# The delta rule's output norm and the out projection of the even layer in one block, the attention's four slices of the contraction first

## The chip, the cores and the metric

The kernel runs on one core of a Trainium2 chip. The time is that of the device for one execution, in microseconds; every comparison is of medians of several executions of the same program.

## The reference, cut to what matters

Two residual layers over a sequence of 1024 tokens of width 1024, all in float32. The even layer ends like this:

```python
def even_layer(x, norm_g, w_in, conv_w, a_log, dt_bias, out_norm, q_gain, k_gain, sinks, w_out, band_bias):
    ...
    o_a = gated_delta_rule(q_a, k_a, v_a, beta_l.astype(F32), alpha_l.astype(F32),
                           a_log.astype(F32), dt_bias.astype(F32))
    o_a = rms_norm(o_a, out_norm) * jax.nn.silu(z_a.astype(F32)).reshape(bsz, T, GDN_HEADS, GDN_HEAD_DIM)
    o_b = sliding_window_attention(...)
    o_b = o_b * jax.nn.silu(z_b.astype(F32))
    mixed = jnp.concatenate([o_a.reshape(bsz, T, BRANCH_WIDTH), o_b], axis=-1).astype(x.dtype)
    return x + mixed @ w_out
```

The delta rule has four heads of 128 channels, the attention eight heads of 64. So `mixed` has 1024 channels: 512 of the delta rule, which need a norm over each head's 128 channels and a gate, and 512 of the attention, which are finished long before. The product with `w_out` sums over all 1024.

## The kernel before

Features lie with channels on the 128 partitions and the 1024 tokens along the free dimension. "Slice" means 128 of the 1024 channels over which the out projection sums; there are eight, `mixed[k]`: four of the delta rule (`v`) and four of the attention (`zb`). A product of float32 operands is made of three passes (L167 to L169) with a high and a low part of each side. For the out projection, ScalarE rounds a slice of the features to its high part (`mh`, L1557) and a slice of the weights to its high part (`wh`, in the tile `xt_hi`, L1559); GpSimd subtracts to get the features' low part (`ml`, L1565), VectorE to get the weights' low part (`wl`, in `xt_lo`, L1596). Each of these is one operation on 128x1024 elements.

The program is a row of blocks. A block holds one list of instructions for each engine, and the next block begins on all engines when the last instruction of the block before is done. Within a block engines wait for each other by semaphores; each engine takes its own list strictly in order. Three blocks matter here:

- `gdn_state` (L1203), the delta rule's recurrence over eight chunks: short matmuls that wait for VectorE and ScalarE in turn. Its last product is the output `o`, which is `v`.
- `norm_blocks` (L612) with tag "eo", the norm of `v`. ScalarE squares the four slices (L655), TensorE sums the squares over the partitions (L675), ScalarE takes the root of the sums (L657), VectorE the reciprocal (L694); the result, one row for each head, is split in a high part (ScalarE, L660) and a low part (VectorE, L698), four operations of 128x256 each; TensorE spreads the rows over 128 partitions by matmuls with a column of ones (L686, L687), two for each half of 512 tokens; and VectorE multiplies slice, gain and the spread row in PSUM (L704). GpSimd meanwhile multiplies the slices with their gates (L666). PSUM has eight banks: bank 0 takes the sums, banks 2 to 7 the spread rows of three slices. At the block's start SP loads the first three rows of weights.
- `project_out` (L1507) with tag "eout". For the first four tiles of 128 tokens the loop over the slices is outside: with slice k ready, TensorE adds its products for tiles 0 to 3 (8 banks, 24 matmuls of 128x512 with all three passes). Then tiles 4 to 7 follow, each with all eight slices. VectorE adds the residual to a finished tile (L1601) and SP stores it. SP loads the weights' rows 3 to 7 one after another into three slots as these come free.

The odd layer's out projection is the same function with `early=4`: it runs beside the end of another computation, which needs two banks, so the first four slices are applied to three tiles only, and tile 3 catches up later.

Where several programs share a block (`side_by_side`, L335), each yields numbers, its due times, and `in_turn` (L308) writes out on each engine whichever is due next:

```python
def in_turn(eng, *programs):
    ...
    while min(due, default=NEVER) < NEVER:
        i = due.index(min(due))
        due[i] = next(steps[i], NEVER)
```

The numbers set the order of an engine's list and nothing else.

## Time and profile before

| | us |
|---|---|
| median of 3 runs | 1574.04 |
| lowest, highest | 1573.94, 1577.53 |
| profiled execution | 1572.04 |
| its span of instructions | 1570.3 |
| mean granted clock of TensorE | 0.897 of full |

The time of an execution is its span and about 1.7 us around it. In the profile PE is TensorE's matmul side, PEld its loading of weights, DVE is VectorE, ACT ScalarE, POOL GpSimd, SP the engine that issues transfers. "PE busy" counts matmuls at whatever clock was granted, so a long busy time is no proof of speed: the clock stands beside it. Matmuls overlap, so the distance between two starts, not the duration of one, is what a matmul costs in a stream. An operation's duration on DVE and POOL includes the time for which it stood waiting after it was issued.

### The profile page before, as it was taken

The numbers are of one execution on the slowest core, as the hardware profiler recorded it, in microseconds if no ns is written. First come the engines' busy times: TensorE is split into PE (matmuls) and PEld (weight loads), VectorE is DVE, ScalarE is ACT, GpSimd is POOL, SyncE is SP. The second block draws the span as 40 slices with busy tenths as digits, with TensorE's granted clock in tenths as the row PEclk, the third lists the DMA queues.
The fourth block names the chain that finished last, engine by engine and source line by source line (L and its number), as shares of the span: only waits on it lengthen the run. The fifth ranks groups of instructions, "written<-read, shape, count | busy, mean of one in ns | idle before, by whom it ended". The sixth has DMA issues, their size and how long they took to land. (4 is left out here: it accounts for less than half of the span.)

```text
span 1570.3 us, 20457 instructions
## 1 busy us (share of the span) xinstructions
PE 1321.9 (84%) x8434; PEld 1102.5 (70%) x8434; DVE 913.7 (58%) x1230; ACT 458.0 (29%) x670; POOL 322.1 (21%) x164
## 2 busy tenths in 40 slices
PE   4999999899568869967997999999432789999698
PEld 4677888678357747856886888887221688988587
DVE  5277745810477446127977464953679777355841
ACT  5234353231333233024342211221652311212310
POOL 2222212121055226013221111121200400000330
PEclk9999999899788989989999999999665666879899
DMA  5212112220400012434241343322000000010423
GB/s 178 42 41 64 44 44 81 68 81 1 154 1 1 1 58 91 147 122 116 81 118 64 102 102 123 86 67 81 0 1 1 1 1 1 2 55 1 188 68 120
DMA packets 118708, 101.96 MB, mean 65 GB/s; under 512 B 37144, under 2 KB 102808, under 8 KB 118488
## 3 DMA queue, kind: packets, MB, share of 16 engines
q1 hardware_dynamic: 104984, 81.65, 17.3%
q10 hardware_dynamic: 13632, 19.01, 3.7%
q8 instruction: 66, 1.08, 0.3%
q14 instruction: 26, 0.21, 0.0%
HBM read 74.43 MB, written 24.51 MB: 63 GB/s over the span
## 5 line engine op out<-in xcount | busy, mean ns | idle before, releaser
L167 PE MATMUL banks<-xt_lo,w_hi 128*128 128x512 f32 x816 | 322.9, 396 | 6.5 <-POOL w_lo L488 6.5
L169 PE MATMUL banks<-xt_hi,w_hi 128*128 128x512 f32 x816 | 319.1, 391 | 0.0
L168 PE MATMUL banks<-xt_hi,w_lo 128*128 128x512 f32 x816 | 319.1, 391 | 0.0
L488 POOL TENSOR_TENSOR w_lo<-features,w_hi 128x1024 fp32r<-128x1024 f32 x55 | 149.0, 2711 | 527.3 <-ACT w_hi L497 527.3
L167 PEld LDWEIGHTS banks<-xt_lo,w_hi 128*128 128x128 f32 x816 | 154.2, 189 | 42.0 <-POOL w_lo L488 7.0
L169 PEld LDWEIGHTS banks<-xt_hi,w_hi 128*128 128x128 f32 x816 | 154.0, 189 | 32.6
L168 PEld LDWEIGHTS banks<-xt_hi,w_lo 128*128 128x128 f32 x816 | 154.4, 189 | 31.3
L541 ACT ACTIVATE temporaries<-banks 128x1024 f32<-128x1024 f32 x47 | 56.0, 1192 | 327.0 <-PE banks L169 318.8
L1601 DVE TENSOR_TENSOR temporaries<-temporaries,banks 128x1024 f32<-128x1024 f32 x16 | 19.5, 1221 | 109.5 <-PE banks L169 100.8
L286 PE MATMUL banks<-temporaries,features 128*128 128x128 f32 x256 | 37.5, 309 | 36.1 <-DVE temporaries L263 36.1
L497 ACT ACTIVATE w_hi<-features 128x1024 fp32r<-128x1024 f32 x55 | 57.8, 1054 | 27.9 <-PE banks L169 26.7
L286 PEld LDWEIGHTS banks<-temporaries,features 128*128 128x128 f32 x256 | 34.8, 220 | 38.8 <-DVE temporaries L263 38.8
L167 PE MATMUL banks<-xt_lo,oout_mh 128*128 128x512 f32 x128 | 51.3, 401 | 11.6 <-DVE xt_lo L1596 11.5
L167 PE MATMUL banks<-xt_lo,eout_mh 128*128 128x512 f32 x128 | 50.9, 398 | 6.8 <-DVE xt_lo L1596 6.8
L2478 DVE COPY_PREDICATED big<-constants,banks 128x384 f32<-128x384 int32 x64 | 34.3, 578 | 32.1 <-PE banks L2418 31.6
L168 PE MATMUL banks<-xt_hi,oout_ml 128*128 128x512 f32 x128 | 51.0, 398 | 0.0
L169 PE MATMUL banks<-xt_hi,oout_mh 128*128 128x512 f32 x128 | 50.8, 397 | 0.0
L168 PE MATMUL banks<-xt_hi,eout_ml 128*128 128x512 f32 x128 | 50.8, 396 | 0.0
L169 PE MATMUL banks<-xt_hi,eout_mh 128*128 128x512 f32 x128 | 50.6, 395 | 0.0
L2418 PE MATMUL banks<-features 64*128 64x128 f32 x384 | 48.9, 332 | 0.0
L588 DVE TENSOR_TENSOR features<-temporaries 128x1024 f32<-128x1024 f32 x13 | 15.9, 1225 | 56.4 <-ACT temporaries L541 56.4
L1596 DVE TENSOR_TENSOR xt_lo<-features,xt_hi 128x1024 fp32r<-128x1024 f32 x16 | 45.5, 2896 | 4.4 <-ACT xt_hi L1559 4.4
(445 smaller groups left out, 2657.8 us busy)
## 6 DMA issues: line engine op xcount, KB each, us to landing
features<-in_even_w_in SPq DMA_DIRECT2D x26, 512.0 KB, 3.9
features<-in_odd_w_in SPq DMA_DIRECT2D x25, 512.0 KB, 4.6
features<-in_x SPq DMA_DIRECT2D x8, 512.0 KB, 7.4
even_gates<-temporaries ACTq DMA_DIRECT2D x8, 512.0 KB, 2.6
features<-even_gates SPq DMA_DIRECT2D x8, 512.0 KB, 8.9
features<-in_even_w_out SPq DMA_DIRECT2D x8, 512.0 KB, 3.5
temporaries<-in_x SPq DMA_DIRECT2D x8, 512.0 KB, 4.0
h_between_layers<-temporaries SPq DMA_DIRECT2D x8, 512.0 KB, 4.1
```

What stands on the lines that cost most here:

```text
L167: nc.tensor.matmul(out, w[0], x[1], start=start, stop=False)
L168: nc.tensor.matmul(out, w[1], x[0], start=False, stop=False)
L169: return nc.tensor.matmul(out, w[0], x[0], start=False, stop=stop)
L286: last = nc.tensor.matmul(co.ps[:, n % 8, k * P:(k + 1) * P], ring[i % deep][:, (4 * h + k) * P:(4 * h + k + 1) * P], diagonal[i % 4], sta ...
L488: nc.gpsimd.tensor_tensor(wl[n % 2], wr[n % NW], wh[n % 2].bitcast(F32), ALU.subtract).then_inc(low, 1)
L497: nc.scalar.activation(wh[n % 2], wr[n % NW], ACT.Copy).then_inc(high, 1)
L541: nc.scalar.activation(to, mine, ACT.Copy, scale=0.5 if kind in ("gate", "turned_gate") else 1.0).then_inc(evacuated, 1)
L588: link(nc.vector.tensor_tensor(dst, x[:, 3:3 + T], x[:, 4:4 + T], ALU.subtract))
L1596: nc.vector.tensor_tensor(wl[:, k, :], wr[k % 3], wh[:, k, :].bitcast(F32), ALU.subtract).then_inc(low_w, 1)
L1601: nc.vector.tensor_tensor(rr[t % 3], rr[t % 3], co.ps[:, 2 * (t % 4):2 * (t % 4) + 2, :].rearrange("p b n -> p (b n)"), ALU.add).then_inc( ...
L2418: last = nc.tensor.matmul(scores(h)[:, i * P:(i + 1) * P], key[rows, j, ct], query[rows, j, ct], start=True, stop=True)
L2478: nc.vector.copy_predicated(x.ring[c % 2][:, h, :, :], mask, scores(h).rearrange("p (s t) -> p s t", s=3)).then_inc(kept, 1)
```

## The change

The block of the norm is gone. A new program `delta_norm` does the same norm inside the block of the out projection. For this:

- the contraction runs over the attention's slices first (`zb + v`, with the rows of `w_out` in the matching order, `first_row`), and the delta rule's slices wait until `delta_norm` has written all eight halves of `v`;
- `project_out` now always works as the odd layer's did: the first four slices go to tiles 0 to 2, in banks 0 to 5, and tile 3 catches up at slice 4. The due times of the first four slices are an argument: `NORM_PACES` in the even layer; `FINISH_PACES` in the odd one, with the numbers that stood in the code;
- `delta_norm` has banks 6 and 7 alone: bank 6 for the sums, then both for the spread rows, a half of 512 tokens in each, so VectorE's last multiplication is split in two halves of 128x512 and TensorE waits for a half before it spreads the next but one;
- squares and rows lie where the weights lay (`A_F[4]`), the weights in `A_F[3]`, which is free once the attention is done, so their first three rows are loaded at the start of `gdn_state`;
- a conversion of the constant `pairs` (L692), which only norms over 64 channels need, is not repeated.

```diff
-def gdn_state(co):
+def gdn_state(co, ahead):
...
+        @block.sync
+        def _(sp):
+            for to, src, sem in ahead:
+                sp.dma_start(to, src).then_inc(sem, 16)
...
-def project_out(co, tag, w, mixed, hi_at, lo_at, res, dst, stored, fetched=False, fetch=(), early=KT, ready=None):
+NORM_PACES = dict(scalar=(0, 4, 7, 9), gpsimd=(0, 4, 7, 10), tensor=(3, 8, 13, 14), vector=(1, 5, 7, 10))
+FINISH_PACES = dict(scalar=(5, 7.5, 10, 12.5), gpsimd=(5, 7.5, 10, 12.5), tensor=(8, 11.5, 15, 18.5), vector=(6, 9.5, 11, 15.5))
+def delta_norm(co, x, gain, gate):
...
+    nc = co.nc
+    Q, N = T // 4, WB
+    here = A_F[4]
+    sq = [co.at(here + 1024 * i, (T,)) for i in range(N)]
+    high, low = (co.rounded(f"eo_rows_{n}", here + 2048 + 1024 * i, (T,)) for i, n in enumerate(("hi", "lo")))
+    rows = co.at(here, (Q,))
+    scale, eps = (co.at(A_CST + C_PARAM + 2 + i, (1,)) for i in range(2))
+    own_quarter = co.at(A_CST + C_QUARTER, (4,))
+    quarters = [(slice(32 * q, 32 * q + 32), slice(Q * q, Q * q + Q)) for q in range(4)]
+    squared, summed, rooted, inverted, high_r, low_r, spread, gated = (
+        co.sem(f"eo_{n}") for n in ("squared", "summed", "rooted", "inverted", "high_r", "low_r", "spread", "gated"))
+    co.delta_normed = normed = co.sem("eo_normed")
+    def scalar(act):
+        yield 1
+        for n in range(N):
+            nc.scalar.activation(sq[n], x[n], ACT.Square).then_inc(squared, 1)
+        yield 8
+        act.wait_ge(summed, N)
+        nc.scalar.activation(rows, co.ps[:, 6, 0:Q], ACT.Sqrt, bias=eps, scale=scale).then_inc(rooted, 1)
+        yield 11
+        act.wait_ge(inverted, 1)
+        for q, (_, of) in enumerate(quarters):
+            nc.scalar.activation(high[:, of], rows, ACT.Copy, scale=own_quarter[:, q:q + 1]).then_inc(high_r, 1)
+    def gpsimd(pool):
+        for n in range(N):
+            yield 2 if n < 2 else 5
+            pool.wait_ge(squared, n + 1)
+            nc.gpsimd.tensor_tensor(x[n], x[n], gate[n], ALU.mult).then_inc(gated, 1)
+    def tensor(pe):
+        yield 4
+        for n in range(N):
+            pe.wait_ge(squared, n + 1)
+            for own, of in quarters:
+                last = nc.tensor.matmul(co.ps[own, 6, 0:Q], co.at(A_CST + C_SUM + 31 - n, (32,)), sq[n][:, of], start=n == 0, stop=n == N - 1)
+            last.then_inc(summed, 1)
+        yield 12
+        pe.wait_ge(low_r, 4)
+        for n in range(N):
+            for h in range(2):
+                if n >= 1:
+                    pe.wait_ge(normed, 2 * n - 1 + h)
+                hs = slice(512 * h, 512 * h + 512)
+                spreader = co.hot_r[:, n:n + 1].to_broadcast([P, P])
+                nc.tensor.matmul(co.ps[:, 6 + h, :], spreader, low[:, hs], start=True, stop=False)
+                nc.tensor.matmul(co.ps[:, 6 + h, :], spreader, high[:, hs], start=False, stop=True).then_inc(spread, 1)
+    def vector(dve):
+        yield 9
+        dve.wait_ge(rooted, 1)
+        nc.vector.reciprocal(rows, rows).then_inc(inverted, 1)
+        yield 11
+        dve.wait_ge(inverted, 1)
+        for q, (_, of) in enumerate(quarters):
+            dve.wait_ge(high_r, q + 1)
+            nc.vector.scalar_tensor_tensor(low[:, of], rows, own_quarter[:, q:q + 1], high[:, of].bitcast(F32), ALU.mult, ALU.subtract).then_inc(low_r, 1)
+        yield 12
+        for n in range(N):
+            dve.wait_ge(gated, n + 1)
+            for h in range(2):
+                hs = slice(512 * h, 512 * h + 512)
+                dve.wait_ge(spread, 2 * n + h + 1)
+                nc.vector.scalar_tensor_tensor(x[n][:, hs], x[n][:, hs], gain, co.ps[:, 6 + h, :], ALU.mult, ALU.mult).then_inc(normed, 1)
+    return dict(scalar=scalar, gpsimd=gpsimd, tensor=tensor, vector=vector)
...
+def project_out(co, tag, w, mixed, hi_at, lo_at, res, dst, stored, paces, ready, w_at, first_row=0, fetched=False, fetch=()):
...
-    wr = [co.at(A_F[4] + 1024 * i, (D,)) for i in range(3)]
+    wr = [co.at(w_at + 1024 * i, (D,)) for i in range(3)]
     rr = [co.at(A_T + 1024 * i, (D,)) for i in range(3)]
+    early = WB
+    w_rows = [slice((first_row + k * P) % D, (first_row + k * P) % D + P) for k in range(KT)]
...
-                sp.dma_start(wr[k], w[k * P:(k + 1) * P, :]).then_inc(loaded[k], 16)
+                sp.dma_start(wr[k], w[w_rows[k], :]).then_inc(loaded[k], 16)
...
-            sp.dma_start(wr[k % 3], w[k * P:(k + 1) * P, :]).then_inc(loaded[k % 3], 16)
+            sp.dma_start(wr[k % 3], w[w_rows[k], :]).then_inc(loaded[k % 3], 16)
...
-            yield 5 + 2.5 * k if k < early else base + k
+            yield paces["scalar"][k] if k < early else base + k
...
-            yield 5 + 2.5 * k if k < early else base + k
+            yield paces["gpsimd"][k] if k < early else base + k
...
-            yield 8 + 3.5 * k if k < early else base + 2 + k
+            yield paces["tensor"][k] if k < early else base + 2 + k
             if k == early:
                 pe.wait_ge(*ready)
                 for k_ in range(early):
                     products(3, k_)
             pe.wait_ge(low_m, k + 1)
             pe.wait_ge(low_w, k + 1)
-            for t in range(3 if k < early < KT else 4):
+            for t in range(3 if k < early else 4):
...
-            yield (6, 9.5, 11, 15.5)[k] if k < early < KT else base + k
+            yield paces["vector"][k] if k < early else base + k
...
+    w_in = [co.sem(f"eout_w{k}", kept=True) for k in range(3)]
     gdn_chunks(co)
-    gdn_state(co)
-    w_in = [co.sem(f"eout_w{k}", kept=True) for k in range(3)]
-    norm_blocks(co, "eo", [(x_, 128, on, za_) for x_, za_ in zip(v, za)], 1,
-                ahead=[(co.at(A_F[4] + 1024 * k, (D,)), a["even_w_out"][0][k * P:(k + 1) * P, :], sem) for k, sem in enumerate(w_in)])
+    gdn_state(co, [(co.at(A_F[3] + 1024 * k, (D,)), a["even_w_out"][0][W + k * P:W + (k + 1) * P, :], sem) for k, sem in enumerate(w_in)])
     out_stored = [co.sem(f"eout_stored{i}", kept=True) for i in range(3)]
-    side_by_side(co, clearing(co, at=100), project_out(co, "eout", a["even_w_out"][0], v + zb, [A_F[0] + 1024 * k for k in range(KT)], [A_F[2] + 1024 * k for k in range(KT)],
-                                                       x, dst, out_stored, fetched=w_in))
+    side_by_side(co, clearing(co, at=100), delta_norm(co, v, on, za),
+                 project_out(co, "eout", a["even_w_out"][0], zb + v, [A_F[0] + 1024 * k for k in range(KT)], [A_F[6] + 1024 * k for k in range(WB)] + [A_F[2] + 1024 * k for k in range(WB)],
+                             x, dst, out_stored, NORM_PACES, (co.delta_normed, 2 * WB), A_F[3], first_row=W, fetched=w_in))
...
-                             co.output_stored, fetch=[(zc[b], oc[b]) for b in range(WB)], early=WB, ready=(co.finish_done, 2)))
+                             co.output_stored, FINISH_PACES, (co.finish_done, 2), A_F[4], fetch=[(zc[b], oc[b]) for b in range(WB)]))
```

GpSimd (POOL) from the start of the norm. Before, the four gates (L666), then, past the border of the blocks (branches), one low part after another; `eout_ml0` is slice 0, `eout_mh0` its high part:

```order
L662 UNCONDITIONAL_BRANCH
L666 TENSOR_TENSOR features_51<-features_51 128x1024 x4
L635 UNCONDITIONAL_BRANCH
L347 UNCONDITIONAL_BRANCH
L1565 TENSOR_TENSOR eout_ml0_4851<-features_51,eout_mh0_4843 128x1024
L1565 TENSOR_TENSOR eout_ml1_4852<-features_51,eout_mh1_4844 128x1024
L1565 TENSOR_TENSOR eout_ml2_4853<-features_51,eout_mh2_4845 128x1024
```

And now, where slice 0 is the attention's:

```order
L347 UNCONDITIONAL_BRANCH
L1651 TENSOR_TENSOR eout_ml0_4746<-features_51,eout_mh0_4738 128x1024
L1551 TENSOR_TENSOR features_51<-features_51 128x1024 x2
L1651 TENSOR_TENSOR eout_ml1_4747<-features_51,eout_mh1_4739 128x1024
L1551 TENSOR_TENSOR features_51<-features_51 128x1024 x2
L1651 TENSOR_TENSOR eout_ml2_4748<-features_51,eout_mh2_4740 128x1024
L1651 TENSOR_TENSOR eout_ml3_4749<-features_51,eout_mh3_4741 128x1024
L1651 TENSOR_TENSOR eout_ml4_4750<-features_51,eout_mh4_4742 128x1024
```

The gates moved behind the first low part and stand in pairs among the others; eight operations stand before slice 4.

VectorE (DVE) from the start of the norm; `xt_lo` is the weights' low part. Before:

```order
L690 UNCONDITIONAL_BRANCH
L692 CAST pairs_64<-constants_49 128x640
L694 RECIPROCAL temporaries_52<-temporaries_52 128x256
L698 SCALAR_TENSOR_TENSOR rows_lo_62<-temporaries_52,constants_49,rows_hi_61 128x256 x4
L704 SCALAR_TENSOR_TENSOR features_51<-features_51,constants_49,banks 128x1024 x4
L635 UNCONDITIONAL_BRANCH
L355 UNCONDITIONAL_BRANCH
L1596 TENSOR_TENSOR xt_lo_54<-features_51,xt_hi_53 128x1024 x8
L1601 TENSOR_TENSOR temporaries_52<-temporaries_52,banks 128x1024 x8
```

Now:

```order
L355 UNCONDITIONAL_BRANCH
L1682 TENSOR_TENSOR xt_lo_54<-features_51,xt_hi_53 128x1024 x3
L1574 RECIPROCAL features_51<-features_51 128x256
L1682 TENSOR_TENSOR xt_lo_54<-features_51,xt_hi_53 128x1024
L1579 SCALAR_TENSOR_TENSOR eo_rows_lo_4737<-features_51,constants_49,eo_rows_hi_4736 128x256 x4
L1586 SCALAR_TENSOR_TENSOR features_51<-features_51,constants_49,banks 128x512 x8
L1682 TENSOR_TENSOR xt_lo_54<-features_51,xt_hi_53 128x1024 x4
L1687 TENSOR_TENSOR temporaries_52<-temporaries_52,banks 128x1024 x8
```

Three subtractions of weights moved ahead of the reciprocal and one ahead of the low parts of the rows (L1579). On TensorE the 18 matmuls of slice 0 now stand ahead of the 16 sum matmuls, the 18 of slice 1 between these and the 16 spreading matmuls (L1568, L1569), and slices 2 and 3 behind the spreading ones.

## Rows read from the trace of the kernel before

**Rows 1.** The page's costliest groups: the projection's first pass. Busy us, mean ns | idle before, releaser.
```profile
L167 PE MATMUL banks<-xt_lo,eout_mh 128*128 128x512 f32 x128 | 50.9, 398 | 6.8 <-DVE xt_lo L1596 6.8
```

**Rows 2.** Busy us (x) by stretch: PE, PEld, DVE, ACT, POOL, then clock, DMA share, GB/s.
```profile
519.80:566.00 46.20, 42.30 (x320) 39.30 (x320) 18.82 (x64) 12.29 (x32) 0.00 (x0) 0.95 0.00 1
566.00:586.00 20.00, 9.32 (x48) 4.99 (x48) 10.88 (x10) 7.53 (x11) 9.29 (x4) 0.66 0.23 80
...
596.00:633.00 37.00, 37.00 (x165) 30.61 (x164) 18.13 (x7) 7.85 (x8) 16.78 (x6) 1.00 0.14 46
```

**Rows 3.** Timeline of the norm's block: start us, us, engine, line, operation [idle before <-releaser].
```profile
566.13 3.90 ACT L655 ACTIVATE temporaries<-features 128x1024 f32<-128x1024 f32 x4 [0.52 <-PEq L1216]
...
567.27 9.29 POOL L666 TENSOR_TENSOR features<-features 128x1024 f32<-128x1024 f32 x4 [47.47 <-ACT temporaries L655]
...
571.94 1.75 DVE L694 RECIPROCAL temporaries<-temporaries 128x256 f32<-128x256 f32 x1 [5.29 <-ACT temporaries L657]
...
574.34 3.69 DVE L698 SCALAR_TENSOR_TENSOR rows_lo<-temporaries,constants,rows_hi 128x256 fp32r<-128x256 f32 x4 [0.65 <-ACT rows_hi L660]
...
578.17 0.76 PE L686 MATMUL banks<-rows_lo,one_hot 128*128 128x512 f32 x1 [7.01 <-DVE rows_lo L698]
```

**Rows 4.** Timeline of the projection's first microseconds, before the change.
```profile
585.92 1.06 ACT L1557 ACTIVATE eout_mh<-features 128x1024 fp32r<-128x1024 f32 x1 [10.49 <-PEq L635]
...
587.06 2.35 POOL L1565 TENSOR_TENSOR eout_ml<-features,eout_mh 128x1024 fp32r<-128x1024 f32 x1 [10.50 <-ACT eout_mh L1557]
...
587.96 2.53 DVE L1596 TENSOR_TENSOR xt_lo<-features,xt_hi 128x1024 fp32r<-128x1024 f32 x1 [2.33 <-ACT xt_hi L1559]
...
589.37 3.36 POOL L1565 TENSOR_TENSOR eout_ml<-features,eout_mh 128x1024 fp32r<-128x1024 f32 x1
...
590.64 0.76 PE L167 MATMUL banks<-xt_lo,eout_mh 128*128 128x512 f32 x1 [6.76 <-DVE xt_lo L1596]
```

**Rows 5.** Timeline of the product stream: two half-clock rows, two full-clock rows, last add.
```profile
591.20 0.63 PE L168 MATMUL banks<-xt_hi,eout_ml 128*128 128x512 f32 x1
...
595.04 0.63 PE L168 MATMUL banks<-xt_hi,eout_ml 128*128 128x512 f32 x1
...
596.49 0.39 PE L167 MATMUL banks<-xt_lo,eout_mh 128*128 128x512 f32 x1
...
610.09 0.39 PE L167 MATMUL banks<-xt_lo,eout_mh 128*128 128x512 f32 x1
...
680.33 1.22 DVE L1601 TENSOR_TENSOR temporaries<-temporaries,banks 128x1024 f32<-128x1024 f32 x1 [9.66 <-PE banks L169]
```

**Rows 6.** One line's instructions: duration ns min/median/max, first and last start.
```profile
L1596 DVE TENSOR_TENSOR xt_lo<-features,xt_hi x16: 1212/3406/3433, 588.0 to 1502.4; 128x1024 fp32r<-128x1024 f32 x16
...
L1565 POOL TENSOR_TENSOR eout_ml<-features,eout_mh x8: 2352/3374/3405, 587.1 to 609.4; 128x1024 fp32r<-128x1024 f32 x8
```

**Rows 7.** Timeline: the first of the four low parts of the norm's rows, alone.
```profile
574.34 2.50 DVE L698 SCALAR_TENSOR_TENSOR rows_lo<-temporaries,constants,rows_hi 128x256 fp32r<-128x256 f32 x1 [0.65 <-ACT rows_hi L660]
```

**Rows 8.** Timeline of the attention: a VectorE operation with an input in PSUM beside GpSimd.
```profile
469.25 0.64 DVE L1446 TENSOR_TENSOR features<-features,banks 128x512 f32<-128x512 f32 x1
...
469.41 1.90 POOL L1487 TENSOR_TENSOR temporaries<-temporaries,constants 128x1024 f32<-128x1024 f32 x1 [0.34 <-DVE constants L1471]
```

**Rows 9.** Busy us by stretch, columns as in group 2: where TensorE's clock rises.
```profile
578.20:581.90 3.70, 3.70 (x9) 2.92 (x10) 1.28 (x1) 0.00 (x0) 0.00 (x0) 0.50 0.01 4
...
590.70:595.50 4.80, 4.80 (x12) 3.73 (x13) 4.80 (x2) 2.71 (x4) 4.80 (x2) 0.50 0.61 197
...
431.90:435.10 3.20, 2.77 (x26) 2.80 (x28) 0.11 (x1) 1.28 (x1) 0.00 (x0) 0.50 0.02 5
435.30:438.50 3.20, 2.14 (x40) 1.90 (x36) 2.66 (x4) 0.00 (x0) 0.00 (x0) 1.00 0.00 0
```

**Rows 10.** Timeline of the odd layer: VectorE goes on while GpSimd waits.
```profile
1232.55 4.96 POOL L2291 TENSOR_TENSOR features<-features 128x1024 f32<-128x1024 f32 x1 [0.75 <-DVE features L2340]
1233.52 1.21 DVE L2335 TENSOR_TENSOR features<-features,big 128x1024 f32<-128x1024 f32 x1
```

More of the change, by code:

```diff
@@ L1524, in project_out @@
         co.sem(f"{tag}_{x}") for x in ("high_w", "high_m", "low_w", "low_m", "multiplied", "added"))
-    base = 20 if early < KT else 0
+    base = 20
     def sync(sp):
```

## The prediction, made before the changed kernel was run

> **What bounds the kernel now.** I read the page's costliest groups first. The out projection of the even layer is the "eout" groups: three passes of 128 matmuls, 384 in all, and before them TensorE stood idle once, 6.8 us, until VectorE had its first low part (L1596) [rows 1]. Then the busy times by stretch: in the norm's own block (566 to 586) TensorE is busy 9.3 of 20.0 us at a mean clock of 0.66, while in the first half of the projection it is busy without a break at 1.00 [rows 2]. So the norm's block is latency and the projection's block is TensorE. The reader should carry two points of the timeline: the norm's block starts its first work at 566.13 [rows 3], the projection's at 585.92 and its first product at 590.64 [rows 4], 4.72 us later. The last add of the projection starts at 680.33 [rows 5]. Between 566.13 and 590.64 lie 24.5 us without one product. That is the stock the change draws on.
>
> **The product stream, priced.** At the full clock 60 matmuls start between 596.49 and 610.09: 0.2267 us each. At the half clock nine start between 591.20 and 595.04: 0.427 each [rows 5]. 384 x 0.2267 = 87.05, some 12 cold ones cost 12 x 0.200 = 2.4, and 0.24 remain to the last add: 590.64 + 89.7 = 680.33, so the stream has no other hole.
>
> **What is moved ahead.** Work for slice 0 now starts with the block, so its first product comes at about 566.13 + 4.72 = 570.9. But only three of the four token tiles go early and banks 6 and 7 serve the norm. Of the four attention slices' 96 matmuls TensorE does, ahead of the spreading matmuls, two slices of three tiles, 36 matmuls; slices 2 and 3 stand behind the spreads in TensorE's queue. So 348 matmuls, 348 x 0.2267 = 78.9 us, still come after the last spread. The end is: time at which TensorE leaves the spreads, plus 78.9, plus 0.24.
>
> **When the spreads can start: the chain on GpSimd.** They wait for the four low parts of the norm's rows (L698 before). These have two SBUF inputs, as have the L1596 operations, and GpSimd's operations read SBUF too. The rows show the two engines taking turns: L1596 takes 1.21 us at least and 3.41 in the median, GpSimd's subtraction 2.35 at least and 3.37 in the median [rows 6]; its first one ran 587.06 to 589.41 while VectorE's, begun at 587.96, ended at 590.49, and GpSimd's next, begun at 589.37, took 3.36 [rows 4]. A low part of 256 columns fared the same: it began at 574.34 behind GpSimd's fourth gate, which ended at 567.27 + 9.29 = 576.56 [rows 3], and took 2.50 [rows 7], and the three after it, with GpSimd out of work, took (3.69 - 2.50) / 3 = 0.40 each [rows 3].
> In the new block GpSimd's queue is: low of slice 0, gates 0 and 1, low of slice 1, gates 2 and 3, lows of slices 2 and 3. All eight find their inputs ready: ScalarE needs about 0.95 us for each operation and has 10 ahead of its wait for the sums, so the parts for slice 2 are there by 576; the one for slice 3 comes after the root, near 580, and is wanted near 589. Alone such an operation costs 9.29 / 4 = 2.32 [rows 3]. Between them VectorE takes its turn with four weight subtractions, 3.37 - 2.32 = 1.05 each, and, with two GpSimd operations queued, with low part 0 and low part 1; parts 2 and 3 come when GpSimd has run out of work. With one turn each, the last low part ends when all of this is done: 567.27 + 8 x 2.32 + 4 x 1.05 + 4 x 0.40 = 591.6. Spreads start at 591.7. Before, they started at 578.17 [rows 3]; 13.5 us of the head start go here.
> TensorE is not what makes them late: slice 0, half cold, ends near 577, the sixteen sum matmuls take about 2 us more, and root and reciprocal, some 2.5 us together as before (the reciprocal of 1.75 ended at 573.7 [rows 3]), are through near 582. Were slice 0 cold to its end, 1.6 us later, and the sums 1.8 us longer, the reciprocal would still beat GpSimd's queue. From 582.9 to 591.7 TensorE idles.
>
> A sentence beside this from the Trainium skill, SBUF — State Buffer, section "Who interferes with whom": a VectorE instruction with two SBUF inputs and a GpSimd one that reads SBUF exclude each other for their whole length. The trace agrees [rows 6, 7]. The page says that issue order decides and not who gets the pair when both are waiting, which is the open question of the first rival.
>
> **The spreads.** Eight pairs of 128x512 matmuls with two banks instead of six, and VectorE's operation split in halves. It has one input in PSUM; such an operation of 128x512 took 0.64 us beside a GpSimd one [rows 8], so it does not take turns; I take 0.69, a little more, for the gain that is multiplied in as well. One bank's round at the half clock: 0.43 + 0.63 for the matmuls, 0.69, and 0.10 of semaphores = 1.85, for two pairs in flight 0.93 per pair; at the full clock 0.23 + 0.40 + 0.69 + 0.10 = 1.42, or 0.71 per pair. The clock is at the half level after such idle time: 0.50 while the spreads began before, from 578.2 to 581.9, and again while the products began, from 590.7 to 595.5 [rows 9]. It rose about 3.7 us after the spreads' start and 4.9 after the products'. So about 4.3 us cold, the rest warm: TensorE leaves 6.5 us after the start, between 5.4 if all were warm and 7.3 if all were cold: 591.7 + 6.5 = 598.2.
>
> **Hidden or zero.** The three weight loads now start with the delta rule's block, some 46 us earlier; SP had nothing there and the transfers' share is 0.00 [rows 2]: 0, with 0.3 either side. Weight row 3 may load from 571 and is wanted after 581. SP's loads of x come first as before. Slices 4 to 7 start on ScalarE at about 600; TensorE has 36 + 24 matmuls, 13.6 us, for cover, GpSimd delivers the first after about 4.5 us and one per 3.4 us against 5.4 us of products. One block fewer saves its barrier, 0.3 us, which is inside the start times used. The odd layer gets the same numbers by another argument: 0.
>
> **The sum.** 598.2 + 78.9 + 0.24 = 677.3 against 680.33: 3.0 us gained. The profiled execution took 1572.04 us, so 1569.0 by the sum; the median of the runs is 1574.04, 2.0 above it, and 3.0 less is 1571.0.
>
> **Rivals.**
> A. VectorE keeps the ports. If the low parts run back to back as soon as gate 3 is done, they end at 567.27 + 6 x 2.32 + 4 x 1.05 + 1.6 = 587.0, 4.6 us sooner, the idle time is short enough that the clock may hold (up to 1.1 more): gain 7.6 to 8.7, time about 1565.8. For it: once VectorE's L2335, issued at 1233.52 while GpSimd had been waiting since 1232.55, ran unhindered in 1.21 us and GpSimd took 4.96 [rows 10]. Against it: all seven contests of the projection went in turns, and the low parts are short, so GpSimd's next operation waits when each ends. 0.25.
> B. The clock comes back late. TensorE's share in the cold spreading loop is 0.86 of 0.93, and the products behind it then run cold for another 3.7 to 4.9 us, 9 to 11 matmuls at 0.20 more, with 0.8 for the loop: about 3 us lost, 1574.0, nothing gained. Against it: TensorE was busy only 2.77 of 3.20 us from 431.9 at 0.50, and from 435.3 it ran at 1.00 [rows 9]. 0.11.
> C. Slower: the clock does not settle at all in the loop with two banks, and slices 2 and 3 and tile 3's catch-up run at half clock. That is 60 x 0.20 = 12.0 lost and 0.8 in the loop: 9.8 slower, 1583.8. It decides against the kernel once over 15 products (3.0 / 0.20) run cold, and past the 0.3% once some 38 do. Nothing in the rows shows products of 128x512 cold for over 4.9 us. 0.04. The Trainium skill, TensorE: Matmul & The Clock Gate, section "A second HAM failure mode: psum-queue depth-cycling", tells of a kernel whose clock went up and down because short pauses between groups of matmuls recurred with the banks; the spreading loop before, with six banks, shows no such thing, and two banks are not in this trace.
>
> **Chances.** Forecast 0.60, of which 0.08 lies beyond 4.7 us of gain; A 0.25; B 0.11; C 0.04. About 0.3%, 4.7 us, is what a measurement of this kernel can tell from no change. Faster 0.08 + 0.25 = 0.33, same 0.52 + 0.11 = 0.63, slower 0.04. The range takes in A at its bottom (1574.0 - 8.7 = 1565.3, and a little) and B with 1 us of spread at its top: 1565.0 to 1575.0.
>
> **What would show it.** In the profile after: first product near 570.9; 36 products, then the sum matmuls; an idle stretch of TensorE of about 9 us before the spreads, ended by the low parts of the rows; in it two low parts of about 2.7 us and a start of the spreads near 591.7 (A: two or three of 0.47 and 587); halves of 0.69 on VectorE; slice 2 from 598; last add near 677.3. Wrong if slices 2 and 3 wait for their low parts, if TensorE waits again at slice 4, or if the delta rule's block is longer than 46.2 us because of the loads in it.

## The result, and the profile after

| | before | after |
|---|---|---|
| median | 1575.09 us (4 runs) | 1591.97 us (4 runs) |
| range | 1573.94 to 1577.53 | 1589.89 to 1592.66, and one at 4412.7 |
| profiled execution | 1572.04 | 1589.89 |
| its span | 1570.3 | 1588.1 |
| granted clock | 0.897 | 0.887 |

The ratio is 1.0101, with an interval of 1.0080 to 1.0121: by it the changed kernel is 1.0%, or 16 us, slower, and the time lies outside the predicted range. A ratio in this document compares only executions within 1.5% of the fastest of their kernel. The one execution at 4412.7, at a granted clock of 1.0, is left out of what follows and was not explained.

In the new block itself things went as forecast. The timeline of the changed kernel, with the columns of [rows 3] (L1643, L1645, L1651 and L1682 are the parts `mh`, `wh`, `ml` and `wl`; L1551 the gates, L1574 the reciprocal, L1579 the rows' low parts, L1568 and L1569 the spreads, L1687 the last add):

```profile
569.55 1.06 ACT L1643 ACTIVATE eout_mh<-features 128x1024 fp32r<-128x1024 f32 x1 [0.52 <-PEq L1216]
...
574.27 0.77 PE L167 MATMUL banks<-xt_lo,eout_mh 128*128 128x512 f32 x1 [5.66 <-DVE xt_lo L1682]
...
581.99 6.68 POOL L1551 TENSOR_TENSOR features<-features 128x1024 f32<-128x1024 f32 x2
...
583.19 1.75 DVE L1574 RECIPROCAL features<-features 128x256 f32<-128x256 f32 x1
...
585.08 1.39 DVE L1682 TENSOR_TENSOR xt_lo<-features,xt_hi 128x1024 fp32r<-128x1024 f32 x1
...
586.39 7.92 DVE L1579 SCALAR_TENSOR_TENSOR eo_rows_lo<-features,constants,eo_rows_hi 128x256 fp32r<-128x256 f32 x4
...
588.63 5.00 POOL L1651 TENSOR_TENSOR eout_ml<-features,eout_mh 128x1024 fp32r<-128x1024 f32 x2
...
594.36 0.80 PE L1568 MATMUL banks<-eo_rows_lo,one_hot 128*128 128x512 f32 x1 [7.54 <-DVE eo_rows_lo L1579]
```
```profile
601.68 0.40 PE L167 MATMUL banks<-xt_lo,eout_mh 128*128 128x512 f32 x1
```
```profile
680.78 1.22 DVE L1687 TENSOR_TENSOR temporaries<-temporaries,banks 128x1024 f32<-128x1024 f32 x1 [9.66 <-PE banks L169]
```

From the block's first work to the last add: 680.78 - 569.55 = 111.23 us, where the kernel before took 680.33 - 566.13 = 114.20 [rows 3, 5]. The gain is 2.97. The block starts 3.42 us later than before; 3.39 of that difference are there once the trace is past 83 us, in work that the change does not touch. So at the last add the two kernels are level, 680.33 and 680.78, and all but 0.45 of the 17.8 us of span come behind it, in the odd layer, whose instructions are the same.

Where most of them come is seen in one line of the odd layer, the 64 masks of its state blocks (line, engine, operation, count: duration ns min/median/max, first and last start). Before and after:

```profile
L2478 DVE COPY_PREDICATED big<-constants,banks x64: 562/581/593, 1255.5 to 1455.2; 128x384 f32<-128x384 int32 x64
```
```profile
L2563 DVE COPY_PREDICATED big<-constants,banks x64: 567/582/594, 1258.5 to 1469.8; 128x384 f32<-128x384 int32 x64
```

Each takes as long as before, but they span 211.3 us, not 199.7: 11.6 of the 17.8 lie between the first and the last of them. Up to the first, 3.0 - 0.45 = 2.55 have come; behind the last, 1588.1 - 1469.8 = 118.3 against 1570.3 - 1455.2 = 115.1, so 3.2. With the 0.45 that makes 17.8. The 2.55 and the 3.2 also come in work that did not change; they were not followed further. The stretches of the same work by the clock (columns as in [rows 2]), before and then after:

```profile
1312.50:1346.60 34.10, 33.38 (x272) 31.29 (x270) 19.57 (x27) 6.25 (x11) 0.94 (x1) 0.50 0.00 1
1346.60:1377.20 30.60, 28.02 (x475) 25.99 (x473) 11.70 (x25) 8.27 (x17) 0.00 (x0) 1.00 0.02 4
```
```profile
1315.90:1326.10 10.20, 10.20 (x51) 9.64 (x50) 7.00 (x7) 0.88 (x2) 0.00 (x0) 0.50 0.00 0
1326.20:1339.70 13.50, 10.03 (x177) 9.19 (x178) 11.27 (x16) 4.99 (x8) 0.94 (x1) 1.00 0.01 1
1339.80:1384.20 44.40, 43.68 (x428) 40.95 (x420) 10.90 (x25) 6.55 (x13) 0.00 (x0) 0.50 0.01 1
1384.30:1391.00 6.70, 5.55 (x86) 5.03 (x85) 2.05 (x3) 1.66 (x4) 0.00 (x0) 1.00 0.00 0
```

Before, some 747 matmuls take 64.7 us: the first 272, which are long, at the half clock of 1.2 GHz, and the following 475, nearly all short, at 2.4. After, 742 take 75.1 us: the long ones run partly at the full clock, where TensorE is busy only 10.03 of 13.50 us and VectorE 11.27, and then 428 mostly short ones at the half clock, 44.4 us, for which the pace before (30.6 / 475) gives 27.6. So by this estimate the half-clock stretch costs 16.8 us where it lies, and some 6 of them are given back just ahead of it: 75.1 - 64.7 = 10.4 are left. The two pages' rows of the granted clock, 40 slices each, before and after, show it in slices 33 to 35: 6 6 8 before, 7 7 5 after. The clock is up sooner, and down where the short matmuls are:

```profile
PEclk9999999899788989989999999999665666879899
```
```profile
PEclk9999999899788989989998999999665677579799
```

What has to be explained is therefore not the block but why the clock falls otherwise 660 us later, in work that did not change.

### The profile page after: what moved, and what is told of

The parts are those of the page before. It is cut to its first block and busy times, and to the rows that moved or that the text cites. A ratio compares the mean times of both kernels' runs of the same rounds, so it can differ in the third digit from the quotient of the medians.

```text
span 1588.1 us, 20445 instructions
## 1 busy us (share of the span) xinstructions
PE 1336.7 (84%) x8434; PEld 1116.5 (70%) x8434; DVE 915.6 (58%) x1233; ACT 457.5 (29%) x670; POOL 321.2 (20%) x164
## 5 line engine op out<-in xcount | busy, mean ns | idle before, releaser
L1687 DVE TENSOR_TENSOR temporaries<-temporaries,banks 128x1024 f32<-128x1024 f32 x16 | 19.5, 1222 | 106.7 <-PE banks L169 97.7
L831 PE MATMUL banks<-features,big 32*32 32x32 f32 (+1 forms) x448 | 23.2, 238 | 32.9 <-DVE features L788 19.4
```

What stands on the lines that cost most here:

```text
L831: mm = lambda out, lhs, rhs: nc.tensor.matmul(out, lhs, rhs, start=True, stop=True)
L1687: nc.vector.tensor_tensor(rr[t % 3], rr[t % 3], co.ps[:, 2 * (t % 4):2 * (t % 4) + 2, :].rearrange("p b n -> p (b n)"), ALU.add).then_inc( ...
```

## The experiments

Two series: one on where the 16 us come from, and one on the chain that sets the block. Fourteen runs in four sets; each set has executions of the kernel before beside it. The sets ran on four chips. Times of one kernel fall in two groups, about 16 us between their middles; so each run gives both, "low" and "high", divided at the widest gap, or at one nearly as wide where the text says so. One execution of each run was profiled, as of the two kernels above, and only of these sixteen is the course of the clock known. Eleven of the twelve high ones among them have the stretch of 44.4 us, and none of the four low ones has it; the rest are placed by their time alone.

### Is it the odd layer's place in time?

Edit, in either kernel: one block between the layers with n copies on ScalarE, all else unchanged.

```diff
+def pause(co, n):
+    nc = co.nc
+    with nc.Block() as block:
+        @block.scalar
+        def _(act):
+            for i in range(n):
+                nc.scalar.activation(co.at(A_F[0] + 1024 * i, (T,)), co.at(A_T, (T,)), ACT.Copy)
 def odd_layer(co, a, x, dst):
+    pause(co, n)
```

The kernel before with one copy and with three:

> The kernel before, with a block between the two layers in which ScalarE makes one copy of 128x1024: everything in the odd layer starts some 1.5 us later, nothing else differs. Theory 1 (the 16 us come from when the odd layer starts relative to the changes of TensorE's granted clock, not from the changed block): the time is not 1575 + 1.5 but jumps by several us in either direction, with the difference in the odd layer's state blocks (1345 to 1410) and a different pattern of half-clock stretches there. Theory 2 (something that the changed block leaves behind slows the odd layer): 1576.5, the clock pattern moved by 1.5 us and otherwise as before.

> As the run before, with three copies: some 3.4 us later. Theory 1: again a jump of its own, anywhere from 1574 to 1595. Theory 2: 1578.5.

The changed kernel with one and with three:

> The changed kernel with one copy between the layers. Theory 1: the odd layer's state blocks change their time by several us against the changed kernel's; a time well below 1591 is possible though work was only added. Theory 2: 1593, since what slows the odd layer is still there.

> The changed kernel with three copies. Theory 1: a time of its own between 1572 and 1597. Theory 2: 1595.

Measured, with the unchanged kernel before beside them in the same set:

| run | low | high | median | ratio, interval |
|---|---|---|---|---|
| kernel before | 24: 1567.0 to 1578.4 | 7: 1584.8 to 1594.2 | 1575.86 | |
| before, 1 copy | 4: 1575.0 to 1579.5 | 6: 1588.2 to 1593.1 | 1589.11 | 1.0067, 1.0022 to 1.0112 |
| before, 3 copies | 6: 1570.2 to 1579.5 | 4: 1592.1 to 1596.8 | 1578.28 | 1.0012, 0.9966 to 1.0057 |
| changed, 1 copy | 6: 1572.7 to 1578.7 | 4: 1584.7 to 1590.1 | 1577.39 | 1.0032, 0.9990 to 1.0074 |
| changed, 3 copies | 6: 1570.4 to 1573.6 | 4: 1582.3 to 1585.9 | 1573.39 | 0.9994, 0.9953 to 1.0036 |

A copy costs about 1 us, the block around it half of one. So with 1.5 us of harmless work the median of the kernel before was 13 us higher, and that of the changed one 9 to 15 us lower (against 1586.09, measured below, or 1591.97). Ten executions are few for this: 6 high of 10 beside 7 of 31 come by chance about once in 20 times, and 4 of 10 beside the changed kernel's 11 of 15 once in 8. What is certain is that the 16 us can come without the changed block: the kernel before has the high group too, in 7 of 31 executions. The profiled executions say the same. The one of the kernel before with one copy shows the late stretch of the changed kernel, and the one of the changed kernel with three copies shows the early one of the kernel before; their windows, and the masks:

```profile
1342.70:1387.10 44.40, 43.68 (x430) 40.95 (x422) 10.82 (x25) 6.54 (x13) 0.00 (x0) 0.50 0.01 1
```
```profile
L2478 DVE COPY_PREDICATED big<-constants,banks x64: 565/582/599, 1261.6 to 1472.8; 128x384 f32<-128x384 int32 x64
```
```profile
1310.60:1344.70 34.10, 33.38 (x272) 31.32 (x270) 19.57 (x27) 6.23 (x11) 0.94 (x1) 0.50 0.00 1
1344.80:1375.50 30.70, 28.11 (x474) 26.07 (x473) 11.87 (x25) 8.22 (x16) 0.00 (x0) 1.00 0.03 6
```
```profile
L2563 DVE COPY_PREDICATED big<-constants,banks x64: 560/581/595, 1253.6 to 1453.4; 128x384 f32<-128x384 int32 x64
```

211.2 and 199.8 us from first mask to last: with a pause each kernel has shown the other's course.

### The changed kernel once more, and the chain in the block

> The changed kernel, unaltered, in more executions. Theory 1 (one and the same half-clock stretch of about 44 us in the odd layer comes or does not come by chance, in either kernel): times in two heaps, one at 1567 to 1577, one at 1584 to 1594, and the lower heap 3 us below the lower heap of the kernel before. Theory 2 (the changed kernel falls into that stretch always): all times at 1588 or above. Both: the changed block takes 111.2 us from its first instruction to the last add, against 114.2 before.

Measured: median 1586.09 over 12 executions, 4 low (1564.7 to 1567.8) and 8 high (1585.0 to 1592.9), beside 35 of the kernel before with the median 1574.97, of which 30 low (1570.0 to 1580.8), 4 high (1587.1 to 1590.7) and one at 1674.5. The block took 111.29 us. So "slower" stands, by 11 us in the median, since the high group comes more often: 8 of 12 beside 4 of 34, which chance gives once in some 1700 times. The low executions, though, are below all of the kernel before in this set: the medians of the low groups are 1565.2 and 1573.3, and 8 us apart rather than the 3 that were expected. What gave the other 5 is not known.

The next three change the chain on which the prediction rested. First, GpSimd holds back its low part of slice 2 until the four low parts of the rows are done:

```diff
+            if tag == "eout" and k == 2:
+                pool.wait_ge(co.delta_low, 4)
             pool.wait_ge(high_m, k + 1)
             nc.gpsimd.tensor_tensor(ml[k] ...
```

> The changed kernel, but GpSimd waits for the four low parts of the rows before it subtracts for slice 2; no work is added or taken away. Theory A (the spreads wait because the low parts take turns with GpSimd on the SBUF ports): low parts 1 to 3 take 0.47 us instead of 2.56, the spreads start 20.8 us after the block's start instead of 24.8, and the block takes about 107 us, or 106 if TensorE's clock holds. Theory B (the low parts are late for their inputs, the root and the reciprocal): 24.8 and 111.2 stay.

Second, the wait stands one step earlier, ahead of the last gate:

```diff
+            if n == 3:
+                pool.wait_ge(low_r, 4)
             pool.wait_ge(squared, n + 1)
             nc.gpsimd.tensor_tensor(x[n], x[n], gate[n], ALU.mult)
```

> The changed kernel, but GpSimd waits for the low parts one operation earlier, before the last gate. Theory A: all four low parts take 0.47 us, spreads 18.5 us after the block's start, TensorE idle for only some 1.5 us before them so that its clock stays full, the block about 103.5 us, the kernel 7 to 8 us below the changed one in executions of the same heap. If the last gate, now later, holds back the multiplications: 1 to 2 us less of that. Theory B: no gain.

Measured in the block: 107.38 and 103.80 us, where the changed kernel has 111.23; the spreads start 20.65 and 18.55 us after the block's first work, not 24.81. The rows of the four low parts, first with slice 2 held back, then with the last gate held back (the changed kernel's is in the timeline above):

```profile
581.66 3.75 DVE L1580 SCALAR_TENSOR_TENSOR eo_rows_lo<-features,constants,eo_rows_hi 128x256 fp32r<-128x256 f32 x4
```
```profile
581.52 1.66 DVE L1582 SCALAR_TENSOR_TENSOR eo_rows_lo<-features,constants,eo_rows_hi 128x256 fp32r<-128x256 f32 x4
583.24 0.50 PE L1571 MATMUL banks<-eo_rows_lo,one_hot 128*128 128x512 f32 x1 [1.28 <-DVE eo_rows_lo L1582]
```

Four low parts take 7.92 us beside three GpSimd operations (one running, two queued), 3.75 beside one, and 1.66, 0.42 each, beside none. In the last case TensorE waits 1.28 us instead of 7.54, and the clock does not fall for the spreads. Their windows with the last gate held back, and in the changed kernel (columns as in [rows 2]):

```profile
583.20:589.20 6.00, 5.02 (x16) 2.49 (x17) 4.41 (x7) 0.00 (x0) 5.94 (x3) 1.00 0.15 59
```
```profile
594.30:598.60 4.30, 4.15 (x8) 2.23 (x8) 2.25 (x4) 0.00 (x0) 0.00 (x0) 0.50 0.00 0
```

The clock is 1.00 in the one and 0.50 in the other. The third edit brings slice 2's products ahead of the spreads in TensorE's order:

```diff
-NORM_PACES = dict(..., tensor=(3, 8, 13, 14), ...)
+NORM_PACES = dict(..., tensor=(3, 8, 11, 14), ...)
```

> The changed kernel with the products of slice 2 ahead of the spreads on TensorE; nothing else. Theory A: slice 2's low part is there 21.6 us after the block's start, its 18 products fill TensorE's idle stretch to about 25.7, so the spreads start 0.9 us later and 18 products fewer follow: about 108 us for the block. If the products run at half clock because of the idle time before them, 2 us more.

Measured: 109.03 us, between the two values expected, and the spreads begin at 27.98, not near 25.7. Slice 2 needed `ml` 2, which GpSimd delivered as late as everything else in that queue, and after the wait its first 10 products ran at the half clock:

```profile
589.85 0.79 PE L167 MATMUL banks<-xt_lo,eout_mh 128*128 128x512 f32 x1 [4.38 <-POOL eout_ml L1651]
590.44 0.63 PE L168 MATMUL banks<-xt_hi,eout_ml 128*128 128x512 f32 x1
```

It saves 2.2 us: TensorE leaves the spreads 34.01 us after the block's first work, 1.9 later than in the changed kernel, but has 18 products, 4.1 us, fewer to do behind them. It doesn't touch the cause.

Of the whole time, in the same set:

| run | block | low | high | median | ratio, interval |
|---|---|---|---|---|---|
| changed, again | 111.29 | 4 | 8 | 1586.09 | 0.9994, 0.9944 to 1.0044, of the lower ones |
| slice 2 held back | 107.38 | 4: 1560.6 to 1569.4 | 5 | 1584.87 | 0.9920, 0.9867 to 0.9972 |
| last gate held back | 103.80 | 2: 1557.5, 1565.8 | 8: 1577.8 to 1586.5 | 1581.06 | 0.9965, 0.9912 to 1.0017 |
| slice 2 ahead | 109.03 | 3: 1567.1 to 1575.4 | 6: 1581.0 to 1589.2 | 1581.72 | 1.0005, 0.9959 to 1.0051 |

(One execution each of the second and fourth, 2022.9 at a granted clock of 0.62 and 1822.0 at 0.70, is left out. In the fourth row the widest gap, 7.0 us, would give 2 low and 7 high; the 1575.4 above it stands with the low ones for its mean clock of 0.895, as the others of that group have 0.898.) The ratios of the first three rows leave high executions out, 4 of 8, all 5, and 5 of 8, and are not what a user of the kernel gets: by the medians all four are slower than the kernel before, though their blocks are 3 to 10.4 us shorter.

### The shorter block, with a pause

If the place in time decides, a pause must move the best of these from the high group to the low one. The held-back gate with one, three and ten copies:

> The changed kernel with the last gate held back behind the low parts (block 103.80 us, 10.4 below the kernel before) and one ScalarE copy of 128x1024 between the layers (about 1.5 us in the earlier runs). The block's own time stays at 103.8. If only the place in time of the odd layer decides how often the 16 us come, the share of high executions (7 to 8 in 10 without the copy) may move; the low ones should then lie at 1557.5 to 1566 plus 1.5, so 1559 to 1567.5, and the high ones 16 above, at 1575 to 1583. If something that the changed block leaves behind decides it, the share stays at 7 or more in 10 with any pause.

> The same with three copies, about 3.4 us. In the changed kernel this pause went with 4 high executions in 10 instead of 11 in 15. Place in time decides: another share than with one copy, low executions at 1561 to 1569. Something left behind decides: 7 or more in 10 high.

> The same with ten copies, about 10 us, so that the odd layer begins within half a microsecond of where it does in the kernel before. This tells the two apart. If the place in time decides, it behaves like the kernel before: about 1 execution in 6 high, the median near 1573 to 1575 and the ratio within 0.3% of 1. If what the changed block leaves behind decides, 7 or more in 10 are high and the median is near 1588. If neither does and the heap is drawn at random by something outside the kernel, the share here is that of the other two.

and, in a further set, three copies once more, two, and four:

> The kernel with the last gate held back and three pause copies once more, unaltered, with more executions. If its 9 low executions of 10 belong to the kernel (to where the odd layer begins), it shows at least 7 in 10 low again, at 1564 to 1572, and a ratio of 0.995 to 0.998 to the kernel before. If they belonged to that chip or that hour, the share falls back towards that of the held-back gate without a pause (2 low of 10) and the median lies near 1580.

> The same with two copies, about 2.4 us. If the share hangs on the length of the pause, it lies between one copy (0 low of 10, 1578 to 1584) and three (9 low of 10, 1564 to 1572): either both heaps, or one of the two pure. Low executions would be at 1562 to 1570, high ones at 1577 to 1583. A heap drawn at random whatever the kernel would give about one in three high.

> The same with four copies, about 4.4 us. [...] If a longer pause by itself keeps the late stretch away, it behaves as three copies do, 1 us longer: low, at 1565 to 1573.

| copies | low | high | median | ratio, interval |
|---|---|---|---|---|
| 1 | 0 | 9: 1577.9 to 1584.3 | 1579.59 | 1.0032, 1.0009 to 1.0055 |
| 2 | 4: 1568.6 to 1571.5 | 6: 1581.0 to 1586.1 | 1581.02 | 1.0009, 0.9982 to 1.0035 |
| 3 | 9: 1564.4 to 1572.2 | 1: 1580.2 | 1569.29 | 0.9977, 0.9955 to 1.0000 |
| 3 again | 10: 1567.8 to 1578.3 | 2: 1588.6, 1589.4 | 1574.58 | 1.0000, 0.9974 to 1.0026 |
| 4 | 5: 1563.5 to 1572.5 | 2: 1579.4, 1586.6 | 1571.88 | 0.9968, 0.9933 to 1.0002 |
| 10 | 6: 1572.0 to 1581.2 | 3: 1591.1 to 1597.3 | 1579.81 | 1.0019, 0.9985 to 1.0053 |

(Left out: 1819.2 at a granted clock of 0.70 with one copy, 1660.8 at 0.785 with ten. With one copy there is no gap over 2.6 us; all nine are called high, as the profiled one has the stretch of 44.4 us. With four the widest gap, 7.1 us, lies above 1579.4 and the next, 7.0, below it.) The kernel before beside them: median 1574.9 and 1575.9, 23 low of 25 (an execution at 1583.3, 3.9 us above the next lower, is called high) and 24 low of 26; over all four sets 101 low, 15 high.

The block takes 103.77 to 103.84 us in all six. Two copies more, 1.9 us, go with 9 low executions of 10 in place of none of 9 in the same set, which chance gives once in some 9000 times, and with 10 of 12 in the next. The masks of the profiled executions with one and with three:

```profile
L2566 DVE COPY_PREDICATED big<-constants,banks x64: 564/581/598, 1249.2 to 1460.3; 128x384 f32<-128x384 int32 x64
```
```profile
L2566 DVE COPY_PREDICATED big<-constants,banks x64: 564/581/595, 1255.1 to 1450.2; 128x384 f32<-128x384 int32 x64
```

The execution with the longer pause starts its masks 5.9 us later and ends them 10.1 us sooner; 195.1 us from first to last, it is shorter than either course above. So the theory that the changed block leaves something behind falls: it wanted 7 in 10 high with any pause. What holds is that where the odd layer begins changes how often the high group comes. But simple forms of it did not hold. By one of them four copies were to behave as one copy does, mostly high: of 7 executions 5 were low, of 9 with one copy none. By another, ten copies, which bring the odd layer to where it is in the kernel before, should give its share, 1 in 6: 3 of 9 were high, too few executions to tell, and the median of 1579.81 was not the 1573 to 1575 expected. Of the repeat with three copies the share came as expected; its low times and its ratio did not.

None of these is shown to beat the kernel before. Three copies had a ratio of 0.9977 in one set and 1.0000 in the next; four had 0.9968, with an interval that reaches 1.0002.

## Why the prediction was wrong, point by point

- **The first product**, 4.72 us after the block's start: 574.27 - 569.55 = 4.72. Right.
- **The chain on GpSimd.** Last low part 25.5 us after the start by the sum, spreads at 25.6; measured 24.81. The mechanism was as told and a little more so: three low parts of 2.56, 2.55 and 2.56 us and one of 0.47, since the last gate, still running, cost VectorE a turn too (the forecast wanted two long ones). The four turns of 1.05 for the weights' low parts were all paid: four of the eight GpSimd operations took 3.33 to 3.39. The term that was too large is the 4 x 0.40 = 1.6 for the rows' low parts. They added some 0.85: the two GpSimd operations that had one of them ahead took 2.52, 0.20 over the 2.32 alone. So the chain was 0.8 early. Rival A, VectorE keeping the ports, is out: its mark was two or three low parts of 0.47. Holding back GpSimd's operations gave 107.38 and 103.80 us, where 107 and 103.5 were expected of turns.
- **TensorE ahead of the spreads.** The prediction's last paragraph has 36 products and then the sum matmuls; as the order of the change says, 18 products stand ahead of the sums and 18 behind, and so they ran. TensorE then stood idle for 7.54 us, where 8.8 were forecast.
- **The rule of the Trainium skill** (SBUF — State Buffer, "Who interferes with whom"), that a VectorE instruction with two SBUF inputs and a GpSimd one that reads SBUF contend: the trace agrees, with 2.56 us beside a GpSimd operation for what takes 0.42 alone. Which of the two goes on when both wait, the runs show as turns: 7.92, 3.75 and 1.66 us for the same four operations.
- **The spreads.** From their start to slice 2: 601.68 - 594.36 = 7.3 us, forecast 6.5; that is the bound given for a loop cold throughout, though the clock was 0.50 only for the first 4.3 us, as said. So the round of the loop was priced too low: VectorE's halves took 0.75, not 0.69, and two pairs at the half clock 596.49 - 594.36 = 2.13, not 1.85. TensorE left the spreads 32.13 us after the start; the forecast was 598.2 - 566.1 = 32.1. Two errors of 0.8 cancel, which is luck.
- **The stream behind them.** 349 matmuls in 79.1 us at 1.00; the forecast was 348 in 78.9.

```profile
601.70:680.80 79.10, 79.05 (x349) 65.12 (x347) 22.20 (x14) 7.81 (x8) 12.44 (x4) 1.00 0.26 87
```

- **What was called hidden or zero.** The weights' loads in the delta rule's block cost nothing: from its first matmul to the next block's first work it takes 46.28 us in both. Slice 4 came in time.
- **The block's gain:** 3.0 forecast, 2.97 measured, as close as that by the luck just named. Rivals B and C, both of which cost the clock in this block, did not come.
- **The step that failed** is the last one of the sum: "the median of the runs is 1574.04, 2.0 above it, and 3.0 less is 1571.0", with "The odd layer gets the same numbers by another argument: 0". A gain in one block was carried to the end on the belief that the 890 us behind it keep their time. They don't: from the last add on the profiled executions took 890 us before and 907.3 after, 10.4 of the difference where a half-clock stretch of 44.4 us fell on short matmuls, and with a pause ahead of the odd layer each kernel has shown the course of the other. The share of the longer course went from 15 in 116 to 11 in 15 (three of the first set and 8 of 12). The list of rivals had none of this sign at this place; rival C sought the slower side in the changed block alone, and 0.04 was far too little.
- **The second error** was in "About 0.3%, 4.7 us, is what a measurement of this kernel can tell from no change". All that stood behind it were three runs within 3.6 us. Of 117 more executions of the kernel before 116 lay from 1567.0 to 1599.3 and one at 1674.5; three runs had by chance shown one group only. With that spread a gain of 3 us is not to be seen without many executions, and the range of 1565 to 1575 was too narrow: moved down by 3 us, 29 of the 116 single executions would still lie above it.

Could the profile of the kernel before have told? Not the share, but the danger. The windows of the odd layer show a clock that is, on the mean, neither up nor down for some 250 us:

```profile
1100.00:1200.00 100.00, 35.71 (x208) 19.49 (x208) 78.95 (x92) 48.95 (x59) 15.39 (x8) 0.62 0.00 0
1200.00:1268.00 68.00, 47.19 (x534) 38.89 (x534) 51.24 (x64) 24.48 (x41) 19.98 (x11) 0.60 0.00 1
1268.00:1345.00 77.00, 70.42 (x539) 66.02 (x539) 52.27 (x85) 11.85 (x24) 0.94 (x1) 0.68 0.00 1
```

Work that sits between the two levels is where a shift of a microsecond can come out as 16. A rival "the odd layer draws another course of the clock" could have been put on the list from such rows, with a price of at most 30.6 us: the 475 matmuls took that long at the full clock, and the estimate is that half the clock at most doubles it.

**What stays open:** what exactly decides between the courses. There are more than two of them, but few. In all but one of the sixteen profiled executions the clock falls to half between the 20th and the 21st of the 64 masks. There it stays for 34.1 us in the one of the kernel before and in those of the changed one with one copy and with three. In the other twelve it stays for 10.2, rises for 13.7 and falls again, for 44.4 us in eleven, begun between 1328 and 1347, and for 3.4 in that of the held-back gate with three copies, first set. In that with four copies (1579.4, "high") it falls sooner, for 68.3 us. The windows of the last two:

```profile
1337.90:1341.30 3.40, 3.40 (x17) 3.40 (x18) 1.15 (x4) 0.00 (x0) 0.00 (x0) 0.51 0.02 5
```
```profile
1284.40:1352.70 68.30, 66.06 (x427) 61.84 (x428) 39.74 (x54) 9.44 (x19) 0.94 (x1) 0.50 0.00 1
```

One thing goes with the course: how far the work has come when the clock falls there. From the start of the 20th mask to the fall it is 0.99 to 1.01 us in the three with 34.1, 1.02 to 1.26 in the eleven with 44.4, and 1.67 in the one with 3.4. That is an order in fifteen profiled executions, with 0.01 us between the first two kinds; no run tested it. How late the odd layer begins does not by itself predict the share. The low executions of three copies lay 4.6 us apart in their medians in the two sets, with the median of the kernel before moved by 1.0; that is not explained either. That dense work in the odd layer would remove the fork was not tried. Nor was it shown that the 3 us by which the changed block is shorter are what moved its own share: three copies, 3.4 us, put the odd layer back to about where it was, and gave 4 high of 10, which neither 11 of 15 nor 7 of 31 rules out.

## What to carry to other kernels

Before a local gain is carried to the end of a program, look for stages behind it whose granted clock lies between the levels: there the time may be no constant but one of a few courses, and the change can alter how often each comes. To tell a change of 3 us from that, compare the block's own time in the traces (111.23, 111.29, 111.25, 111.24 us in four runs whose medians were 1592, 1586, 1577 and 1573), take ten executions or more, and put a harmless pause of a microsecond or two between the stages as a control: a verdict that such a pause overturns is no verdict on the edit. And where short VectorE operations on a critical chain have to pass a queue of long GpSimd ones, make GpSimd wait for them: that was worth 7.4 us of the block here.

## What the runs showed of the hardware that was not expected

- One program on one core has two groups of times, about 16 us apart: the kernel before 101 low to 15 high, the changed one 4 to 11. In the profiled executions they differ in where a stretch of half clock falls, not in how long VectorE's masks take (0.58 us in the median in all).
- The order of the engines' turns is regular enough to sum with: a VectorE operation of 0.42 us took 2.55 to 2.56 in each of the three turns of the changed kernel, behind GpSimd operations that take 2.3 alone.
- Rarely an execution is far out: 1660.8, 1674.5, 1819.2, 1822.0 and 2022.9 us had mean granted clocks of 0.785, 0.781, 0.702, 0.70 and 0.62. The 4412.7 had 1.0, so a low clock is not its cause; what is, was not found.
